# The first MLP split into two phases: the up product by seven block products for eight, its result through memory, and the weight sums on GpSimd

## The reference, cut to what matters

```python
    h = h + mixed                                   # mixed = attention and convolution @ w_out
    hn = rms_norm(h, norm_mlp_w[layer])
    h = h + jnp.square(jax.nn.relu(hn @ w_up[layer])) @ w_down[layer]   # 1024 -> 4096 -> 1024
```

```python
    mod = jax.nn.silu(c) @ w_ada + b_ada            # a row of 1024 by 1024 x 6144: 48 tiles of 128 columns
```

## Time and profile before

| what | before |
|---|---|
| runs shown | 3472.42, 3479.16 and 3482.66 us, median 3479.16 |
| span of the profiled execution (first to last instruction) | 3475.1 us |
| what lies around the span, by the median | 4.1 us |
| PE busy | 3418.8 us, 98% of the span |
| POOL, DVE, ACT busy | 1220.9, 1586.9 and 983.6 us |
| first MLP on PE | from 479.38 to 1190.80 us |

### The profile page before, as it was taken

The page is one execution under the profiler, slowest core; times in us unless marked ns, Lnnn a source line. Parts: engine busy times, 40 slices in busy tenths (PEclk is TensorE's granted clock), DMA queues, the critical chain, the costliest instruction groups (busy, mean ns, idle before and its releaser), DMA issues.

```text
span 3475.1 us, 39075 instructions
## 1 busy us (share of the span) xinstructions
PE 3418.8 (98%) x16826; PEld 2784.5 (80%) x16826; DVE 1586.9 (46%) x1671; ACT 983.6 (28%) x1441; POOL 1220.9 (35%) x646
## 2 busy tenths in 40 slices
PE   8999999999999999999999999999999999999998
PEld 6887888888888878765788888888888788888887
DVE  5553343333333558486545445445645531222224
ACT  5432221111111221385332222222333432222222
POOL 3112324444444223413323344444322343333333
PEclk9999999999999999999999999999999999999999
DMA  3112312222222311210211222222211111111113
GB/s 111 37 49 70 118 49 79 87 83 91 91 88 91 100 67 49 79 60 1 79 49 49 74 91 82 79 94 73 95 43 43 67 56 49 49 49 49 49 49 127
DMA packets 89431, 242.93 MB, mean 70 GB/s; under 512 B 13334, under 2 KB 20262, under 8 KB 89132
## 3 DMA queue, kind: packets, MB, share of 16 engines
q1 hardware_dynamic: 89260, 240.44, 19.9%
HBM read 222.40 MB, written 18.00 MB: 69 GB/s over the span
## 4 chain that ended last, share of the span: by engine, by line
PE 94%; DVE 3%; ACT 2%; POOL 1%; issue 0%; DMA 0%; POOLq 0%; SPq 0%; DVEq 0%; ACTq 0%
PE ps L618 29%; PE ps L621 28%; PE ps L619 28%; PE ps L790 1%; PE ps L1028 1%; PE ps L1077 1%; PE ps L648 1%; PE ps L1061 1%; PE ps L650 1%; PE ps L649 1%; DVE P L2356 1%; ACT T L1619 0%; PE ps L1014 0%; PE ps L992 0%; PE ps L981 0%; PE ps L686 0%
## 5 line engine op out<-in xcount | busy, mean ns | idle before, releaser
L2736 POOL TENSOR_TENSOR wlo<-raw,whi 128x1024 fp32r<-128x1024 f32 (+3 forms) x367 | 697.1, 1900 | 1728.5 <-ACT whi L1299 1728.5
L618 PE MATMUL ps<-HH,whi 128*128 128x512 f32 (+2 forms) x2736 | 1080.1, 395 | 6.4 <-POOL HL L2742 3.1
L619 PE MATMUL ps<-HL,whi 128*128 128x512 f32 (+2 forms) x2736 | 1069.3, 391 | 0.0
L621 PE MATMUL ps<-HH,wlo 128*128 128x512 f32 (+2 forms) x2736 | 846.9, 391 | 0.0
L1299 ACT ACTIVATE whi<-raw 128x1024 fp32r<-128x1024 f32 (+3 forms) x367 | 309.7, 844 | 1618.4 <-PE ps L621 1419.8
L618 PEld LDWEIGHTS ps<-HH,whi 128*128 128x128 f32 (+2 forms) x2736 | 513.0, 187 | 118.5 <-POOL HL L2742 3.5
L621 PEld LDWEIGHTS ps<-HH,wlo 128*128 128x128 f32 (+2 forms) x2736 | 512.7, 187 | 112.2 <-issue 0.6
L619 PEld LDWEIGHTS ps<-HL,whi 128*128 128x128 f32 (+2 forms) x2736 | 512.9, 187 | 108.9 <-issue 2.0
L618 PE MATMUL ps<-GH,whi 128*128 128x512 f32 x1512 | 594.3, 393 | 0.6 <-POOL wlo L2736 0.6
L619 PE MATMUL ps<-GL,whi 128*128 128x512 f32 x1512 | 588.4, 389 | 0.0
L621 PE MATMUL ps<-GH,wlo 128*128 128x512 f32 x1512 | 466.1, 389 | 0.0
(11 more groups left out here) (386 smaller groups left out, 2929.2 us busy)
## 6 DMA issues: line engine op xcount, KB each, us to landing
raw<-in_w_up SPq DMA_DIRECT2D x76, 512.0 KB, 3.2
raw<-in_w_in SPq DMA_DIRECT2D x70, 512.0 KB, 3.2
raw<-in_w_fc SPq DMA_DIRECT2D x64, 512.0 KB, 3.2
raw<-in_w_down SPq DMA_DIRECT2D x104, 256.0 KB, 2.6
raw<-in_w_ada SPq DMA_DIRECT2D x48, 512.0 KB, 3.3
raw<-in_w_fc SPq DMA_DIRECT2D x64, 256.0 KB, 2.6
X<-in_xT SPq DMA_DIRECT2D x16, 512.0 KB, 7.1
raw<-in_w_out SPq DMA_DIRECT2D x16, 512.0 KB, 3.2
```

The costliest lines, as they stand in the source:

```text
L618: e.matmul(o_[0:m, half(hf)], whi_[:, k, :], hi[k0 + k][:, half(hf)], start=first, stop=False)
L619: e.matmul(o_[0:m, half(hf)], whi_[:, k, :], lo[k0 + k][:, half(hf)], start=False, stop=False)
L621: i = e.matmul(o_[0:m, half(hf)], wlo_[:, k, :], hi[k0 + k][:, half(hf)], start=False, stop=last)
L2736: e.tensor_tensor(wlo_of(name), raw_of(name), whi_of(name).bitcast(F), SUB).then_inc(*po.inc("lo " + name))
```

## The change

The MLP now runs in two phases.

**Up phase.** Two up tiles a and b are one pair n (0 to 15), and their product with the activations is a product of 2x2 blocks: output blocks a and b, input channels 0-511 and 512-1023, tokens 0-511 and 512-1023. In place of eight block products of 4 channel blocks each there are seven (`PARTS`: p1, p5, p6, p2, p7, p4, p3), each 4 blocks x 3 = 12 matmuls of 512 columns (`fast`). Their weight operands are the four blocks and four sums of them (`fast_sums`, 4 POOL instructions of 128x512; for pair 0 on DVE), and each is split into a high part by ACT (`fast_hi`, ring WH of four) and a low part by POOL (`fast_lo`). The activation operands, seven blocks of 128x4x512 with high and low parts (OH, OL), are made once, around the end of the w_out product. DVE puts the output together (`fast_step`, nine instructions of 128x512 a pair), ACT squares it, and SP writes it to memory (`hsc`, 512 KB a tile).

**Down phase.** 32 dn tiles (4 groups of 8) with 8 blocks each, 128x1024, in place of 64 with 4. The hidden tiles are read back from memory into HF or GF, 8 for a group; ACT makes the high part and POOL the low part, one hidden tile beside each dn tile of the group before. All 48 ada tiles now lie in this phase, two and one in turn at each dn tile (`ADAS`).

The core of the diff:

```diff
-ADA_AT = sorted([n for n in range(4, 88) if (n - 4) % 12 in (0, 1, 2, 5, 7, 9)] + [15, 27, 39, 51, 63, 75])
+ADAS = [[3 * (n // 2) + i for i in ((0, 1) if n % 2 == 0 else (2,))] for n in range(32)]
+
+PARTS = ("p1", "p5", "p6", "p2", "p7", "p4", "p3")
 
...
-    mlp("w_up", "w_down", "up", "dn", [4] * 8, aux=[(f"ada{m}", d["w_ada"][m]) for m in range(48)], aux_at=ADA_AT)
+    for m in range(32):
+        plan(f"up{m}", d["w_up"][m])
+    for n in range(32):
+        g, m = divmod(n, 8)
+        plan(f"dn{g}_{m}", d["w_down"][m, :, 1024 * g:1024 * g + 1024])
+        for f in ADAS[n]:
+            plan(f"ada{f}", d["w_ada"][f], split=False)
     w = d["w_in2"]
...
+            def fast(t, n, ready=None, between=None):
+
+                bx, bz, by, bw = corners(t, n)
+                bank = {"p1": bx, "p2": bx, "p5": bz, "p3": bz, "p6": by, "p7": by, "p4": bw}
+                for j, p in enumerate(PARTS):
+                    w = 7 * n + j
+                    q.wait_ge(*po(f"{t}lo {n} {p}"))
+                    if p == "p2":
+                        q.wait_ge(*ac(f"{t}s {n}"))
+                    elif p == "p7":
+                        q.wait_ge(*dv(f"{t}u2 {n}"))
+                    elif p == "p3":
+                        q.wait_ge(*dv(f"{t}c22a {n}"))
+                    elif n:
+                        q.wait_ge(*dv({"p1": f"{t}c11 {n - 1}", "p5": f"{t}c12a {n - 1}", "p6": f"{t}u3 {n - 1}", "p4": f"{t}c21a {n - 1}"}[p]))
+                    wh, wl_ = WH[w % 4][:].rearrange("p (k m) -> p k m", k=4), part(t, n, p)[1].rearrange("p (k m) -> p k m", k=4)
+                    for k in range(4):
+                        if between:
+                            between(p, k)
+                        if ready:
+                            for tok in ready(p, k):
+                                q.wait_ge(*tok)
+                        e.matmul(bank[p], wh[:, k, :], OH[p][:, k, :], start=k == 0 and p not in ("p2", "p7", "p3"), stop=False, skip_group_check=True)
+                        e.matmul(bank[p], wh[:, k, :], OL[p][:, k, :], start=False, stop=False, skip_group_check=True)
+                        i = e.matmul(bank[p], wl_[:, k, :], OH[p][:, k, :], start=False, stop=k == 3, skip_group_check=True)
+                    freed_ = {"p2": pair_of(t, n)[:1], "p4": pair_of(t, n)[1:]}.get(p, ())
+                    i.then_inc(*pe.inc(f"{t}{n} {p}", *freed_))
 
...
+            for n in range(16):
+                fast("up", n, ready=None if n else ready2, between=None if n else norm2)
+            for n in range(32):
+                g, j = divmod(n, 8)
+                if (g, j) == (3, 0):
+                    lend("n3 sq")
+                job(f"dn{g}_{j}", ghs if g % 2 else hhs, gls if g % 2 else hls, lambda k: [either(f"dnl {8 * g + k}")], 8)
+                row_step(n)
...
                     elif ridx[name] >= 2:
@@ -1365,6 +1464,39 @@
...
+                for x in tok:
+                    q.wait_ge(*x)
+                if w > 3:
+                    q.wait_ge(*pe(f"{t}{(w - 4) // 7} {PARTS[(w - 4) % 7]}"))
+                e.activation(WH[w % 4][:], part(t, n, p)[0], ACT.Copy).then_inc(*ac.inc(f"{t}hi {n} {p}"))
...
+                for j in range(7):
+                    if 7 * n + j + 3 > 3 and 7 * n + j + 3 < 112:
+                        fast_hi("up", 7 * n + j + 3)
+                    if n and j == 0:
+                        fast_square("up", n - 1, 1)
+                    elif j == 1:
+                        fast_s("up", n)
+                        if n:
+                            fast_square("up", n - 1, 0)
...
+                    elif (n, j) == (15, 5):
+                        highs(widx["dn0_0"])
+                    elif (n, j) == (15, 6):
+                        for k in range(4, 8):
+                            high(f"dnh {k}", HF[:, k, :], HH[:, k, :], dma[f"hr{k}"](f"hr {k}"), pe("up15 p4"))
+            fast_square("up", 15, 1)
+            fast_square("up", 15, 0)
 
             def mlp(up, dn, sizes, norm, pre, bias=None, first_copy=None, after=None, on_last=None, rt_free=()):
 
...
+            for n in range(32):
+                g, j = divmod(n, 8)
+                highs(widx[f"dn{(n + 1) // 8}_{(n + 1) % 8}"] if n < 31 else widx["gg0"])
+                if g < 3:
+                    f = 8 * g + 8 + j
+                    k = 8 * (1 - g % 2) + j
+                    high(f"dnh {f}", (HF if g % 2 else GF)[:, j, :], (HH if g % 2 else GH)[:, j, :], dma[f"hr{k}"](f"hr {f}"))
+                elif j:
+                    on_last3(j - 1)
+            on_last3(7)
...
+
+            def fast_step(t, n, p, relu, last=False):
+
+                bx, bz, by, bw = corners(t, n)
+                ha, hb = hidden(n)
+                q.wait_ge(*pe(f"{t}{n} {p}"))
+                if p == "p6":
+                    q.wait_ge(*ac(f"{t}s {n}"))
+                    if n > 1:
+                        q.wait_ge(*dma[f"h{2 * (n % 2)}"](f"{t}h {2 * n - 4}"))
+                    tt(ha[:, half(1)], hb[:, half(1)], by, ADD, f"{t}u2 {n}")
+                elif p == "p2":
+                    finish(ha[:, half(0)], bx, 0, relu, f"{t}c11 {n}")
+                elif p == "p7":
+                    tt(hb[:, half(0)], hb[:, half(1)], by, ADD, f"{t}u3 {n}")
+                    q.wait_ge(*dv.now())
+                    tt(hb[:, half(1)], hb[:, half(0)], bz, ADD, f"{t}c22a {n}")
+                    q.wait_ge(*dv.now())
+                    finish(hb[:, half(1)], hb[:, half(1)], 1, relu, f"{t}c22 {n}")
+                elif p == "p4":
+                    tt(hb[:, half(0)], hb[:, half(0)], bw, ADD, f"{t}c21a {n}", *([f"free {t} yw"] if last else []))
+                    q.wait_ge(*dv.now())
+                    finish(hb[:, half(0)], hb[:, half(0)], 0, relu, f"{t}c21 {n}")
+                elif p == "p3":
+                    tt(ha[:, half(1)], ha[:, half(1)], bz, ADD, f"{t}c12a {n}", *([f"free {t} xz"] if last else []))
+                    q.wait_ge(*dv.now())
+                    finish(ha[:, half(1)], ha[:, half(1)], 1, relu, f"{t}c12 {n}")
...
+
             for m in range(8):
                 q.wait_ge(*dma[f"x{m}"]("load2"))
+                if m == 7:
+                    square_sum("n2", 6)
+                    fast_sums("up", 0)
                 to_x(f"wo{m}", m, f"x2 {m}")
-                if m:
-                    weigh("hl2", m - 1, col("norm_mlp", m - 1))
+                if 0 < m < 5:
+                    operand5(m - 1)
+                if m > 3:
+                    g = col("norm_mlp", m)
+                    q.wait_ge(*dv.now())
+                    stt(OF["p6"][:, m - 4, :], X[:, m, half(1)], g, OF["p5"][:, m - 4, :], MUL, SUB, f"o6f {m - 4}")
+                    q.wait_ge(*dv.now())
+                    stt(OF["p4"][:, m - 4, :], X[:, m, half(0)], g, OF["p6"][:, m - 4, :], MUL, SUB, f"o4f {m - 4}")
+                if 0 < m < 7:
                     square_sum("n2", m - 1)
-            weigh("hl2", 7, col("norm_mlp", 7))
+            q.wait_ge(*pe("wo7"))
+            fast_sum4("up", 0)
             square_sum("n2", 7)
...
+                q.wait_ge(*dma[f"w{widx[a] % 4}"](a))
+                q.wait_ge(*dma[f"w{widx[b] % 4}"](b))
+                if n > 1:
+                    q.wait_ge(*pe(f"{t}{n - 2} p3"))
+                a1, a2, b1, b2 = raw_of(a)[:, half(0)], raw_of(a)[:, half(1)], raw_of(b)[:, half(0)], raw_of(b)[:, half(1)]
+                s1, s2, s4 = (part(t, n, p)[0] for p in ("p5", "p6", "p3"))
+                tt(s1, b1, b2, ADD, f"{t}s5 {n}")
+                tt(b1, b1, a1, SUB, f"{t}s7 {n}")
+                q.wait_ge(*po(f"{t}s5 {n}"))
+                tt(s2, s1, a1, SUB, f"{t}s6 {n}")
+                q.wait_ge(*po.now())
...
+            fast_lo("up", 0)
+            fast_lo("up", 1)
+            operand_low("p5", 3, dv("o6f 3"))
+            operand_low("p6", 3, dv("o4f 3"))
+            operand_low("p4", 3)
+            fast_lo("up", 2)
+            fast_lo("up", 3)
+            for i in range(4):
+                operand_low("p7", i)
+            fast_lo("up", 4)
+            fast_lo("up", 5)
+            for i in range(4):
+                operand_low("p3", i, dv(f"o7f {i}"))
+            fast_lo("up", 6)
+            fast_sums("up", 1)
+            for w in range(7, 112):
+                if w % 7 == 5 and w < 105:
+                    fast_sums("up", w // 7 + 1)
+                fast_lo("up", w)
+            for k in range(4):
+                low(f"dnl {k}", HF[:, k, :], HH[:, k, :], HL[:, k, :], ac(f"dnh {k}"))
+            lows(widx["dn0_0"])
 
 
...
+            for n in range(32):
+                g, j = divmod(n, 8)
+                lows(widx[f"dn{(n + 1) // 8}_{(n + 1) % 8}"] if n < 31 else widx["gg0"])
+                if g < 3:
+                    low(f"dnl {8 * g + 8 + j}", (HF if g % 2 else GF)[:, j, :], (HH if g % 2 else GH)[:, j, :], (HL if g % 2 else GL)[:, j, :], ac(f"dnh {8 * g + 8 + j}"))
+                for f in ADAS[n]:
```

(20 more changed lines are left out.)

227 lines of the change are left out of this document (198 added, 29 removed).

## The result

The changed kernel takes **3565.58 us** (median; 3565.14 to 3566.18) beside 3478.76 us for the kernel before: ratio 1.0246 with a 95% interval of 1.0231 to 1.0262, so 87 us slower. The prediction was 3500 with a range to 3532. The mechanism that it named for the down phase is there, but it costs 108 us, more than twice the 48 that I put down.

What follows compares the result with a forecast made beforehand. PE was taken to bound the kernel, with no waits, so late operands show in full. Span 3475.1 - 43.5 (fewer matmuls) + 16 (start) + 48 (down phase) = 3495.6, plus 4.1 around it: 3500 us, range 3470 to 3532.

Steps and rivals of the forecast that it cites:

- -43.5 for the fewer matmuls: Up phase on PE: 84 matmuls for 96 a pair, 192 fewer over 16 pairs at 0.2267 us, -43.5 us.
- 0 for the steady up phase: Up phase after its start: POOL, DVE and ACT keep within PE's 19.04 us a pair, so no added time.
- its loop: Down phase: closed loop from POOL low part to low part through ada product, reduction and load, 12.9 us a tile; PE needs 11.3.
- rival 3: Down phase: POOL's second ada product also keeps out DVE's reduction; 12 steps grow by 1.9, +22, so 3522 us; chance 13%.
- Rivals 1, 2 and 4: 1: loop does not hold PE, 3457, 14%; 2: part of it, 3474, 13%; 4: up phase held by POOL, 3515, 8%.
- +48, the down phase: Down phase: PE gaps from the closed loop, late reloads and the seam, together 48 us, range 30 to 55.
- load issued to ACT's high part 3.11: Down phase loop: link from issue of a 512 KB load to ACT's high part, taken as 3.11 us.
- some 0.5 us late: Odd down-phase steps: reload lands beside the second ada load, ACT's hidden high part some 0.5 us late, 12 x 0.5 = 6.
- 37 + 6 + 1 = 44: Down phase: 23 loop steps x 1.6 = 37, late hidden high parts 6, dn tile 2 late by 1.
- The seam: Between up and down phase: dn tile 0's low part stands behind four hidden low parts on POOL, +4 us.
- The start: Pair 0 of the up phase: PE waits for POOL's queue before p6, p7, p3 and pair 1, +16 us, range 11 to 25.
- rival 5: Down phase: gaps of 1.6 us in 13 lower PE's clock, 46 us more, 3546 us; chance 4%.

Runs made afterwards that it cites:

- Run 5: Changed kernel, each reload a step earlier but issued behind its step's loads: 3565.33 us; then changed kernel, dn loads reading whole w_up tiles in place of w_down: 3535.91 us.
- run 4: Changed kernel with SP's reload of each hidden tile issued one step earlier, two in a group's first step: 3536.45 us, ratio 1.017 to the kernel before.
- run 9: The last combined form (ada first, new start and seam orders, last reduction moved; 3454.34 us) with p6's weights earlier on ACT and POOL: 3455.30 us.
- run 2: Changed kernel with POOL's ada products of a step before the hidden tile's low part: 3479.05 us, ratio 1.0003 to the kernel before.
- run 3: Changed kernel with POOL's ada products of a step also ahead of the next dn tile's low part: 3466.97 us, ratio 0.9972 to the kernel before.

## Why the prediction was wrong

**Right.** -43.5 for the fewer matmuls and 0 for the steady up phase: from 540 to 800 PE is full at clock 1.00. The seat of the loss, its loop and its order: the same links, gaps put down to POOL's low part up to dn tile 25 and only small ones behind it, though they alternate (4.2 to 6.3 us, then none to 1.4) where I had 1.6 before each. The reductions start on time and take 1.95 us each beside POOL's second ada product (3.90 for two), so rival 3 adds nothing. Rivals 1, 2 and 4 did not happen. One count ahead of the prediction is off: by the order of its stream, 28 of the 96 loads of w_up and w_down waited for a reduction in the kernel before, not about 23 of 74. That most of them waited for PE stands.

**The step that failed** is the term "+48, the down phase", by two of its parts:
- "load issued to ACT's high part 3.11". That row was of a w_up tile, which is read whole. A dn tile of this size did not exist before, and lands in 4.1. Measured 4.06 and 4.21, so 0.95 and 1.10 more, about 25 us over twelve double steps. Run 5 shows that 0.8 of the 0.95 and 0.3 of the 1.10 come from the pieces 16 KB apart; the cause of the rest stays open. The rule of the Trainium skill, "DMA: Bandwidth & Descriptors", Anatomy of one DMA, is stated there for DMAs issued by GpSimd; its estimate of 3.2 us does not agree with SP's load of a dn tile, and the measured 4.06 and 4.21 decide.
- "some 0.5 us late" for the hidden high part in the odd steps. I had the issue right (2.27 us behind the dn tile's, predicted 2.3), and 0.5 us late allows the reload some 3.6 us from issue to ACT. It needs 6.5 (1016.07 to 1022.60), and POOL waits 2.35. That the dn tile and the second ada tile, in flight with it, make it so long is argued; run 5 shows only that it shrinks when the dn tile is read whole. That is 1.85 more than predicted, 22 us over twelve; run 4 put the whole lateness at 29.

Both together are 3.9 us a double step, the difference of 30.2 and 26.3, or 47 us. From dn tile 0 to dn tile 25 the phase took 1189.73 - 813.34 = 376.4 us for 25 tiles of 11.3, so 93.9 too many where I had 37 + 6 + 1 = 44: these 50 are the two parts and 3 us in the first tiles. The remaining 10 of the 60 lie at the ends. The seam took 6.7 for 4, and behind tile 25 seven tiles took 86.3 us for 79.1. Of these 7.2, 3.1 are the last wait, which I had not followed: the last ada product stands behind a low part on POOL (it ends at 1273.6), and the reduction behind it. Two gaps of 0.69 and the slow start of tile 25 (see the clock below) make most of the rest. I had written that 0.5 us on a link is 11 us of time, and took a range of 30 to 55 all the same; its upper end rested on no row for a landing under load.

**The start** was +16 and is +23.5. The gaps are smaller than mine (1.58 + 3.29 + 4.57 + 3.76 = 13.2 for 16.3), with one before p1 of pair 0 that I missed and none before p3. The other 10 us are the clock: 0.74, 0.84 and 0.90 in the three windows. I had that as the far end of the range and chose the near one. This tells where PE's time went, not what a full clock would have given: in run 9 the clock came back in part and the time stayed. In the down phase I took a single gap of 3.10 us without a fall as evidence, and my gaps were 1.6. One gap was too little to go by: in run 4 a gap of 3.01 us (before 1022.56) was followed by matmuls at the usual distance, and one of 2.54 us (before 1161.49) by 3 us of matmuls at 1.2 GHz.

**The clock (rival 5, 4%) fell**: 0.90 from 813 to 1080. The tile behind a gap of 5.5 us starts with about 4.9 us of matmuls 0.43 us apart, twice the usual distance, so at 1.2 of 2.4 GHz. The Trainium skill, "TensorE: Matmul & The Clock Gate", HAM oscillation, tells of a kernel in which every wait of a loop for its next data is followed by such a fall; the trace agrees, with 0.90 for 1.00 at these waits of some 5 us. But in this phase it cost next to nothing, and so the price of that rival was wrong too: the tile at 1007.61 takes 13.6 us in place of 11.3, and the loop gives it 13.8. The 2.3 us come out of the gap before the next tile, which is 0.20. With the loop shortened (run 2) or opened (run 3) the clock is back at 1.00 by itself. That the fall is a consequence and not a cause in the down phase is argued from the loop's links, none of which waits for PE in this stretch; no run held the clock alone.

## What to carry to other kernels

Where a buffer's release hangs on work that stands in order behind the next user of the same ring, write the loop down link by link and put what releases a buffer first on every engine that it passes: here putting the ada products ahead of one low part on POOL was worth 87 us, and ahead of both 99, with the same work. A link that is a transfer must be priced by a row of that transfer's own shape and under the traffic of the new schedule; where no row has both, the range has to be wide (here the reload took 6.5 us for a row of 3.1). And a gap that is removed should be expected at the next thing in the queue (seam, last wait, p7), so an edit's value is known only once the wait behind it has been looked at.

## What the runs showed of the hardware

- 512 KB in 4 KB pieces 16 KB apart landed in 4.1 us, the same in whole tiles in 3.6 under this traffic, and the loads beside it went from 4.4 to 3.4 us and from 6.2 to 4.8 (medians of the changed kernel and of the whole-tiles run).
- A reduction of 128x1024 on DVE is not held up by a POOL row of two SBUF operands (1.95 us beside it, 1.99 alone), while a scaled multiply of 128x512 with two SBUF inputs (T<-T,RT, at 510.94 in the changed kernel) took 4.60 us beside POOL's sums, where 33 of the same between 540 and 800 took 1.12 on average and some of them 0.69.
- Gaps of some 5 us every 30 us went with a granted clock of 0.90 (813 to 1080); gaps of 0.2 to 0.8 us every 23 us (run 2, 820 to 1180) left it at 1.00. In between the length of the gap did not tell: 3.01 us without a fall, 2.54 us with one (run 4).
